# Attention in a one-core diffusion step: the next head's query load, key load and maxima are moved within the head

## What is computed

```
q = (rmsnorm(pq, g_q) @ w_uq).reshape(B, T, 8, 64 + 32)
q_rope = apply_rope(q_rope, cos, sin)
kv = (ckv_keys @ w_ukv).reshape(B, K, 8, 64 + 64)
s = q_nope @ k_nope + q_rope @ k_rope            # per head
p = softmax(s * (96 ** -0.5), axis=-1)
o = p @ v
```

## Time and profile before

| | |
|---|---|
| time, median of three runs | 2309.86 us |
| the profiled execution: its time | 2307.95 us |
| the profiled execution: span of the core | 2306.2 us |
| mean granted TensorE clock over the span | 0.961 of 2.4 GHz |
| PE busy over the span | 2129.4 us, 92% |
| DVE, ACT, POOL busy over the span | 950.9, 670.6, 779.2 us |
| stage B, first unit to first score product | 813.1 to 903.0 us |
| the eight heads | 903.0 to about 1201 us |

### The profile page before, as it was taken

How to read it: one execution, slowest core, us unless ns; L and a number is a source line. 1 busy time by engine, 2 the same in 40 slices (tenths; PEclk the granted TensorE clock), 3 DMA queues, 4 the chain that set the end, 5 groups by cost and what they waited for, 6 DMA issues and landing times. The chain is left out here.

```text
span 2306.2 us, 28013 instructions
## 1 busy us (share of the span) xinstructions
PE 2129.4 (92%) x11544; PEld 1956.2 (85%) x11544; DVE 950.9 (41%) x1372; ACT 670.6 (29%) x929; POOL 779.2 (34%) x507
## 2 busy tenths in 40 slices
PE   7499999999999978888878978999999999999995
PEld 2489999999999967767668967999999999999994
DVE  3603444444233036535434417533343344423438
ACT  1234232323222243555555221212111211112120
POOL 0325252616123223434331642323222332223334
PEclk9599999999999989999998989999999999999998
DMA  6365111111211374131318342211111111111113
GB/s 231 110 210 82 35 51 36 55 41 58 72 45 44 101 203 126 42 82 42 82 43 221 118 164 88 77 55 46 46 37 37 55 38 46 37 46 46 42 69 128
DMA packets 189103, 183.88 MB, mean 80 GB/s; under 512 B 52743, under 2 KB 156896, under 8 KB 188976
## 3 DMA queue, kind: packets, MB, share of 16 engines
q1 hardware_dynamic: 187680, 177.37, 25.9%
q0 software_dynamic: 1296, 4.72, 0.5%
HBM read 141.32 MB, written 40.74 MB: 79 GB/s over the span
## 5 line engine op out<-in xcount | busy, mean ns | idle before, releaser
L129 POOL TENSOR_TENSOR s_w_lo<-s_w_raw,s_w_hi 128x1024 fp32r<-128x1024 f32 x86 | 219.6, 2554 | 514.5 <-ACT s_w_hi L124 514.5
L821 PE MATMUL s_psum<-h_hi,s_w_hi 128*128 128x384 f32 x1008 | 346.1, 346 | 25.1 <-POOL h_lo L250 25.1
L2436 PE MATMUL s_ps<-h_hi,s_w_hi 128*128 128x384 f32 x1056 | 353.1, 334 | 0.7 <-ACT gate_pad L2280 0.7
L2436 PE MATMUL s_ps<-h_hi,s_w_lo 128*128 128x384 f32 x1056 | 352.9, 334 | 0.0
L2436 PE MATMUL s_ps<-h_lo,s_w_hi 128*128 128x384 f32 x1056 | 352.8, 334 | 0.0
L821 PE MATMUL s_psum<-h_lo,s_w_hi 128*128 128x384 f32 x1008 | 339.3, 340 | 0.0
L821 PE MATMUL s_psum<-h_hi,s_w_lo 128*128 128x384 f32 x1008 | 339.2, 340 | 0.0
L821 PEld LDWEIGHTS s_psum<-h_hi,s_w_hi 128*128 128x128 f32 x1008 | 191.7, 191 | 35.3 <-issue 19.1
L2436 PEld LDWEIGHTS s_ps<-h_hi,s_w_hi 128*128 128x128 f32 x1056 | 198.3, 188 | 1.4 <-issue 1.0
L2436 PEld LDWEIGHTS s_ps<-h_lo,s_w_hi 128*128 128x128 f32 x1056 | 198.3, 188 | 0.4
L2436 PEld LDWEIGHTS s_ps<-h_hi,s_w_lo 128*128 128x128 f32 x1056 | 198.3, 188 | 0.0
(11 more groups left out here) (362 smaller groups left out, 3799.3 us busy)
## 6 DMA issues: line engine op xcount, KB each, us to landing
s_w_raw<-in_w_ffn_in SPq DMA_DIRECT2D x44, 512.0 KB, 3.7
s_w_raw<-in_w_in SPq DMA_DIRECT2D x41, 512.0 KB, 3.9
s_w_mod<-in_w_mod SPq DMA_DIRECT2D x8, 2048.0 KB, 8.0
w_raw<-in_w_ffn_out SPq DMA_DIRECT2D x11, 1024.0 KB, 4.9
scratch_gates<-sig SPq DMA_DIRECT2D x48, 192.0 KB, 1.9
merge_gates<-scratch_gates SPq DMA_DIRECT2D x16, 576.0 KB, 3.8
w_mod<-in_w_mod SPq DMA_DIRECT2D x4, 2048.0 KB, 10.2
scratch_o_mla<-o_raw SPq DMA_DIRECT2D x8, 576.0 KB, 7.5
```

Source lines behind the costliest of these rows:

```text
L129: pool.tensor_tensor(flat[0], flat[1], flat[2], ALU.subtract).then_inc(self.lo_ready, 1)
L821: return pe.matmul(bank(j), wx[c % 2][:, k, :], hx[:, k, j * CH:(j + 1) * CH], start=(k == 0 and n == 0), stop=(k == KD - 1 and n == 2))
L2436: mm = pe.matmul(ps[bank][:, 0:CH], a[s][:, k, :], b[:, k, j * CH:(j + 1) * CH], start=n == 0, stop=n == 3 * KD - 1)
```

## The change

The item D is cut in two, `Dk` (keys) and `Dq` (queries), and E is called `Dv`.

- **Query load.** `Dq` of head h+2 stands behind `G` of head h+1, just after score tile 6; it stood behind value product 8. `H` moves ahead of score tile 2 and thus ahead of its exp on ACT; it stood behind it.
- **Key load.** `Dk` of head h+2 stands behind score tile 9; it stood behind value product 8.
- **Maxima.** The items M start behind value product 0 (they stood ahead of it) and then come two and two, P behind value product 4, C ahead of value product 5.
- **Stage B.** The keys of heads 2 and 3 are made ahead of the first queries. The split of `w_uq` is done in two parts, heads 0 and 1, then heads 2 to 7, and by single k slices: 30 ACT instructions in place of 5 and 6 POOL instructions in place of 1, over the same elements. The maxima of head 0 start four units later, two behind each of six units and then one behind each of eight.

```diff
     units = [("k", 0, u) for u in range(3)] + [("v", t, 0) for t in range(10)]
+    units += [("k", 1, u) for u in range(3)]
     for h in range(HEADS):
         units += [("q", h, u) for u in range(3)]
-        if h % 2 == 0 and h < HEADS - 2:
+        if h in (2, 4):
             units += [("k", h // 2 + 1, u) for u in range(3)]
...
-FIRST_TOPS = {B_UNITS[B_AT["q", 2, 0] + n]: n for n in range(len(TOP_UNITS))}
+FIRST_TOPS = {}
+for _n in range(len(TOP_UNITS)):
+    FIRST_TOPS.setdefault(B_UNITS[B_AT["q", 2, 0] + 4 + (_n // 2 if _n < 12 else _n - 6)], []).append(_n)
 HEAD_ITEMS = (
-    ("L", 0), ("S", 2), ("H", 0), ("L", 1), ("M", 0), ("M", 1), ("V", 0), ("M", 2),
-    ("S", 3), ("L", 2), ("M", 3), ("M", 4), ("V", 1), ("M", 5),
...
-    ("S", 6), ("L", 5), ("M", 12), ("M", 13), ("V", 4), ("M", 14), ("M", 15),
-    ("S", 7), ("L", 6), ("G", 0), ("P", 0), ("P", 1), ("V", 5), ("C", 0),
+    ("L", 0), ("H", 0), ("S", 2), ("L", 1), ("V", 0), ("M", 0), ("M", 1),
+    ("S", 3), ("L", 2), ("M", 2), ("M", 3), ("V", 1), ("M", 4), ("M", 5),
...
+    ("S", 6), ("L", 5), ("G", 0), ("Dq", 0), ("M", 14), ("M", 15), ("V", 4), ("P", 0), ("P", 1),
+    ("S", 7), ("L", 6), ("C", 0), ("V", 5),
     ("S", 8), ("L", 7), ("T", 0), ("V", 6),
-    ("S", 9), ("L", 8), ("V", 7), ("L", 9), ("V", 8), ("D", 0), ("V", 9), ("E", 0),
+    ("S", 9), ("Dk", 0), ("L", 8), ("V", 7), ("L", 9), ("V", 8), ("V", 9), ("Dv", 0),
     ("S", 10), ("S", 11))
...
-                    if n == 6:
-                        split_uq_hi()
-                    if n == 12:
-                        split_uq_rot()
+                    if n == 4:
+                        act.wait_ge(uq_loaded, 16)
+                        split_uq_hi(0)
+                    if n == 6:
+                        split_uq_rot(0)
+                        split_uq_hi(1)
+                    if n == 13:
+                        split_uq_rot(1)
```

More of the change, by code:

```diff
@@ L1383 @@
 B_RING = 6
+UQ_PARTS = (slice(0, 2), slice(2, HEADS))
 class HeadTops:
@@ L1548, in walk @@
                 if (kind, x, u) == ("q", 0, 2):
-                    item("D", 0, 0)
-                    item("E", 0, 0)
+                    item("Dk", 0, 0)
+                    item("Dq", 0, 0)
+                    item("Dv", 0, 0)
                 if (kind, x, u) == ("q", 1, 2):
@@ L1554, in walk @@
                 if (kind, x, u) == ("q", 3, 2):
-                    item("D", 0, 1)
-                if (kind, x, u) in FIRST_TOPS:
-                    item(*TOP_UNITS[FIRST_TOPS[kind, x, u]], 0)
+                    item("Dk", 0, 1)
+                    item("Dq", 0, 1)
+                for n in FIRST_TOPS.get((kind, x, u), ()):
+                    item(*TOP_UNITS[n], 0)
             item("S", 0, 0)
             item("S", 1, 0)
-            item("E", 0, 1)
+            item("Dv", 0, 1)
             for h in range(HEADS):
                 for kind, u in HEAD_ITEMS:
-                    if kind in "DE":
+                    if kind[0] == "D":
                         if h < HEADS - 2:
@@ L1594, in unit, with load_k @@
                         sp.dma_start(io["q"][x * QH:(x + 1) * QH, :], qst[x % 2][0:QH, :]).then_inc(q_stored[x % 2], 16)
-                def load_qk(h):
+                def load_k(h):
                     e = h % 2
@@ L1602, in load_qk, with load_q @@
                         sp.dma_start(dst[e][0:64, :].bitcast(F32), io[name][h * 64:(h + 1) * 64, :]).then_inc(k_loaded[e], 16)
-                    sp.wait_ge(q_stored[e], 16 * (h // 2 + 1))
+                def load_q(h):
+                    sp.wait_ge(q_stored[h % 2], 16 * (h // 2 + 1))
                     if h >= 1:
@@ L1622, in item @@
                     e = h % 2
-                    if kind == "D":
-                        load_qk(h)
-                    if kind == "E":
+                    if kind == "Dk":
+                        load_k(h)
+                    if kind == "Dq":
+                        load_q(h)
+                    if kind == "Dv":
                         load_v(h)
@@ L1665, in unit @@
                     if kind == "q":
-                        if (x, u) == (0, 0):
-                            pe.wait_ge(uq_ready, 1)
+                        if u == 0 and x in (0, 2):
+                            pe.wait_ge(uq_ready, x // 2 + 1)
                         cols = slice(x * P, (x + 1) * P)
@@ L1727, in _, with split_uq_hi, split_uq_rot @@
             def _(act):
[L1728 to L1740, removed]
+                def split_uq_hi(part):
+                    heads = UQ_PARTS[part]
+                    raw = uq_raw[:, :, :].rearrange("p k (h n) -> p k h n", n=QH)[:, :, heads, :]
+                    hi = uq_hi[:, :, :].rearrange("p k (h n) -> p k h n", n=P)[:, :, heads, :]
+                    for k in range(3):
+                        act.activation(hi[:, k, :, 96:112], raw[:, k, :, 80:96], ACT.Copy, scale=-1.0)
+                        act.activation(hi[:, k, :, 112:128], raw[:, k, :, 64:80], ACT.Copy)
+                        last = act.activation(hi[:, k, :, 0:96], raw[:, k, :, :], ACT.Copy)
+                    last.then_inc(uq_hi_ready, 1)
+                def split_uq_rot(part):
+                    lo = uq_lo[:, :, :].rearrange("p k (h n) -> p k h n", n=P)[:, :, UQ_PARTS[part], :]
+                    act.wait_ge(uq_lo_ready, part + 1)
+                    for k in range(3):
+                        act.activation(lo[:, k, :, 96:112], lo[:, k, :, 80:96], ACT.Copy, scale=-1.0)
+                        last = act.activation(lo[:, k, :, 112:128], lo[:, k, :, 64:80], ACT.Copy)
+                    last.then_inc(uq_ready, 1)
                 def unit(kind, x, u):
@@ L1852, in _, with split_uq_lo @@
                 r = slice(64, 96)
[L1854 to L1858, removed]
+                def split_uq_lo(part):
+                    heads = UQ_PARTS[part]
+                    raw = uq_raw[:, :, :].rearrange("p k (h n) -> p k h n", n=QH)[:, :, heads, :]
+                    hi, lo = [t[:, :, :].rearrange("p k (h n) -> p k h n", n=P)[:, :, heads, 0:QH] for t in (uq_hi, uq_lo)]
+                    pool.wait_ge(uq_hi_ready, part + 1)
+                    for k in range(3):
+                        last = pool.tensor_tensor(lo[:, k, :, :], raw[:, k, :, :], hi[:, k, :, :], ALU.subtract)
+                    last.then_inc(uq_lo_ready, 1)
                 def unit(kind, x, u):
@@ L1880, in item @@
                                            ALU.subtract).then_inc(lo_pool, 1)
-                split_uq_lo()
+                split_uq_lo(0)
+                split_uq_lo(1)
                 walk(unit, item)
```

## The result

| | before | changed |
|---|---|---|
| median of the runs, us | 2307.77 (4 runs, 2305.25 to 2310.9) | 2272.27 (4 runs, 2270.71 to 2273.32) |
| profiled execution, us | 2307.95 | 2273.02 |
| its span, us | 2306.2 | 2271.2 |

The ratio is 0.9847 with a 95% interval of 0.9832 to 0.9862: the changed kernel is faster by some 35 us. In the prediction two references to groups are exchanged: the DVE groups that it calls rows 9 stand above as the earlier trace rows, and the first maximum and first score product that it calls rows 12 stand as the earlier trace rows.

The account below looks back on a forecast made before the run. PE, busy 92% of the span, was taken as the bound, so only its stalls and slow-clock stretches could give time. 2307.95 - 35.1 (heads) + 2.5 (stage B) = 2275.35, plus 1.91 to the runs' median: 2277 us, range 2269 to 2284.

Parts of the forecast that it names:

- Heads: In seven heads, PE's 4.5 us wait for the queries' copy H goes, with the slow matmuls behind it; 35.1 us saved.
- The mis-sized term: At each head's start PE loses 1.27 us in place of 6.28, saving 5.0 us; bounds 3.4 to 5.3.
- Moving only the copy would give little; the load has to move too: In the heads, the query load landing at about 987.6 also held the copy H, so both must move; no size given.
- Stage B: First score product of head 0 at about 905.5 instead of 902.98: 2.5 us lost; bounds 4.4 gained to 5.5 lost.
- the rotation of head 0's queries: In stage B, ahead of the first maximum M0, this rotation comes 3.4 us later.
- the chain from this store to the end of H: In stage B, from the store of head 0's queries over their load to the copy's end: unchanged at 9.7 us.
- My bound on the losing side: In stage B, busier transfers in head 0's query chain could make the start 3 us worse, 5.5 us lost.
- The second rotation: In stage B, six added small ACT instructions of 96 elements at 0.2 us each: 1.2 us.
- DVE as the bound of this stretch: In stage B behind M0, DVE's remaining 34.5 us of work limits what is won back, until 900.4.
- (a): Rival: in each head two short waits close together keep the clock at 0.50; 2288.7 us; chance 0.11.
- (b): Rival: in the heads the key load, or something else, ends the wait, so M0 starts as before; about 2312 us; chance 0.03.
- (c): Rival: the query load delays the maxima's rows, so S0 waits, 7.7 us in each of six heads; 2323.5 us; chance 0.06.

Follow-up runs that it names:

- copy_late: The changed kernel with the copy H back behind score tile 2 on ACT, the query load still early; 2292.03 us, ratio 0.9940 to before.
- maxima_first: The changed kernel with the first two rough score products ahead of value product 0, as before; 2285.84 us, ratio 0.9913 to before.
- heads_alone: The kernel before with only the new order inside the heads, on the old stage B, weight split and first maxima; 2267.15 us, ratio 0.9837 to before.
- load_late: The changed kernel with the query load back behind the key load and the maxima's rows, the copy H still early; 2273.68 us, ratio 0.9867 to before.
- heads_split_parts: heads_alone with the weight split and its waits in two parts; 2269.58 us, ratio 0.9840 to before.

## Why the prediction was right

**Heads: the mechanism held at every step, its size by 2.6 us.** H ran ahead of exp 2, V0 covered it, and the lost time of head 2 is 1.38 us where I had 1.27; M0 stands 6.87 us behind S0, where I had H's end at 6.82; S0 to S0 is 33.06 us against 33.2. The seven short waits at M0 that I had at 0.3 us have no row of PE; they are seen on the weight loads, up to 0.6 us, and in the 0.3 us that PE loses between V0 and M0. The data were there sooner than I had: the early load lands after 3.7 us (median of the eight), not 6.1 as in the place of before. copy_late, maxima_first and heads_alone show that copy, order and clock are the parts of it.

**The mis-sized term** is the saving of a head: 5.0 us predicted, 37.7 / 7 = 5.4 measured. What was wrong is the price before, not the one after. I had read the slow phase behind the stall at head 2 alone: 1.63 us of slow matmuls. The windows of the kernel before, behind the stalls of heads 0, 2 and 3 (columns as above), show that it isn't the same everywhere:

```profile
913.00:921.00 8.00, 7.77 (x23) 6.19 (x24) 3.19 (x5) 1.59 (x3) 1.86 (x1) 0.64 0.01 2
989.00:997.00 8.00, 6.48 (x21) 5.23 (x22) 2.94 (x5) 2.63 (x4) 3.15 (x2) 0.79 0.18 72
1028.00:1036.00 8.00, 7.45 (x20) 5.95 (x21) 2.54 (x4) 1.29 (x2) 2.18 (x1) 0.57 0.11 46
```

Head 2, with 0.79, is among the shortest; head 3 has 0.57. From S0 to S0 head 3 took 39.3 us where head 2 took 38.0. The mean of the seven was 38.6 us ((1173.41 - 902.98) / 7). In the changed kernel it is 33.2 (34.5 for head 0, 33.05 for the others), and the difference of 5.4, taken over all seven, is what was measured. The range of the forecast, 2269 to 2284, is also some 0.8 us too high at both ends: its bounds add up to 2268.3 (2309.86 - 37.2 - 4.4) and 2283.2 (2309.86 - 32.2 + 5.5).

**"Moving only the copy would give little; the load has to move too"** was wrong in its second half, and very likely in its first, which no run tests by itself. I had taken the landing at about 987.6 for a bound, but H could not have begun before 987.32 in any order. In the new order it begins 5.7 us behind S0, and a load issued at S0 is then still nearly in time: load_late lost 1.8 us, not most of the gain.

**Stage B: near in sum, not in its steps.** M0 came 51.1 us behind the stage's start; predicted were 863.9 - 813.1 = 50.8. S0 came 91.8 us behind it, against 905.5 - 813.1 = 92.4. But two steps ahead of M0 are wrong, and their errors cancel. I had the rotation of head 0's queries 3.4 us later; their store came 2.0 us later (850.59 - 810.9 = 39.7 us behind the stage's start, where it was 850.76 - 813.1 = 37.7). And I had the chain from this store to the end of H unchanged at 9.7 us; it took 11.4 (850.59 to 861.98), because the load took 6.2 us from its issue at 854.60 to H where it had taken 5.0. In the six profiles with the new stage B this chain takes 9.9 to 12.5 us, in the four with the old order 9.5 to 10.1. That the sum to M0 is right is luck. My bound on the losing side had named busier transfers for this chain, at 3 us; that they are the cause is not shown.

The second rotation, which I priced at 1.2 us for six instructions, took 1.04. A 32 element instruction of the split and the first row of the rotation:

```profile
818.84 0.22 ACT L1743 ACTIVATE uq_hi<-uq_raw 128x32 fp32r<-128x32 f32 x1
...
842.55 0.27 ACT L1752 ACTIVATE uq_lo<-uq_lo 128x96 fp32r<-128x96 f32 x1
```

The page "ScalarE: Activation LUTs" of the Trainium skill (section "What ACT_TABLE_LOAD costs") gives by its formula, as an estimate, 0.21 and 0.27 us for these two, and 1.0 us for the six. The trace agrees, with 0.22, 0.27 and 1.04 us.

Behind M0 one thing was missing in my steps: the second wait of 2.08 us at the third maximum, with the clock at 0.50 around it. It stands in all six kernels with the new stage B (1.0 to 2.1 us) and in none with the maxima one by one. I had DVE as the bound of this stretch, but DVE was busy for less of it than before, not more (32.30 us against 35.05), and PE too (37.24 against 40.55). From M0 to S0 it took 40.7 us where I had 905.5 - 863.9 = 41.6, and 42.4 before. Which of the parts of stage B costs the 2 us or more isn't settled: the split in two parts alone costs nothing that can be seen (heads_split_parts), and the keys ahead of the queries and the maxima in pairs weren't tried one by one.

**The rivals.** (a) The clock stayed up: 1.00 over all heads. How near it was, heads_alone shows, which has the same head order. In its head 0 PE waits 1.29, 1.11 and 0.70 us, as in head 0 of the changed kernel (1.29, 1.10 and 0.69), but the clock falls:

```profile
902.98 1.22 PE L1726 MATMUL ps_o<-p_hi,v_hi 128*128 128x512 f32 x2 [0.70 <-DVE p_lo L1852]
```

```profile
903.00:906.00 3.00, 3.00 (x7) 2.42 (x8) 0.00 (x0) 2.97 (x4) 2.26 (x1) 0.50 0.75 170
```

It costs about 1 us there (35.4 us from S0 to S0, 34.5 in the changed kernel), and the other heads stay at 1.00. With the single waits of copy_late and maxima_first, 2.1 and 2.5 us, the clock falls in three of six and four of seven heads. (b) No wait for keys showed. (c) The rows of maxima were issued 5.7 us behind the query load, and even three times its traffic there cost nothing.

## What to carry to other kernels

Where one wait of an engine recurs in each turn of a loop, look for work that is already in order behind it and does not need the awaited result. Here the value product of the turn itself was enough, together with an earlier copy. Each alone gave about half, because each leaves a wait of 2 to 2.5 us, and with it the lower clock in part of the turns.

Price a stall with what the clock does behind it, and take that from all its occurrences, not from one: with the same 4.5 us wait one head took 38.0 us and the next 39.3.

Once the large wait is gone, read the waits again. The 12 us of short ones that were left were worth 8 us by the medians, 11 in the heads, by setting one more score tile ahead.

## What the runs showed of the hardware

The clock of TensorE does not fall at one length of a wait in these kernels. A wait of 2.1 us was followed by the lower level in three of six heads, 2.5 us in four of seven (the same wait, the same matmuls around it), 4.5 us in all seven. Short waits do not exclude it either: behind waits of 1.3, 1.1 and 0.7 us within 7 us, at the start of head 0, the clock stayed at 1.00 in the changed kernel and fell to 0.50 for 3 us in heads_alone. And the time at the lower level varied from head to head behind the same 4.5 us wait, as the means of 0.79 and 0.57 above show. The page "TensorE: Matmul & The Clock Gate" of the Trainium skill (section "Part 1: The HAM clock gate") says that the gate's timing runs free of the kernel; that one and the same wait lowers the clock in one head and not in the next agrees with it.

A second thing: two transfers of 432 KB each, put on the queue that carries the maxima's rows 5.3 us ahead of them, moved the time by less than the measurement can tell.

A third: the same load of 432 KB took 6.1 us from issue to landing (median of eight) where it was issued right behind the keys and ahead of the values, 6.0 us in load_late, which puts it back there, and 3.7 us in its early place.
